# Exponentials of the next attention item placed in the first of two groups; the opening squares and the last rows rearranged

## What is computed

```python
proj = rmsnorm(x, g_in) @ w_in             # split into queries, keys, values, SiLU paths, merge gates
y_a = sliding_window_sink_attention(...)   # 8 heads, window of 2 chunks of 64, a sink logit per head
y_b = sparse_attention(...)                # indexer scores, the 256 best keys of each query, 8 heads
y_c = cross_attention(q, mem keys, mem values)          # 4 heads, 256 keys
u = each y * silu(its z) @ w_branch
merged = sum(sigmoid(gates) * u)
out = rmsnorm(x + merged @ w_out, g_final)
```

## Time and profile before

| | us |
|---|---|
| median of 3 runs (lowest, highest) | 2812.31 (2811.92, 2814.73) |
| the profiled execution | 2818.59 |
| its span, first to last instruction | 2816.8 |
| mean granted TensorE clock, share of full speed | 0.972 |

### The profile page before, as it was taken

The page is one execution under the profiler, slowest core; times in us unless marked ns, Lnnn a source line. Parts: engine busy times, 40 slices in busy tenths (PEclk is TensorE's granted clock), DMA queues, the critical chain, the costliest instruction groups (busy, mean ns, idle before and its releaser), DMA issues.

```text
span 2816.8 us, 37280 instructions
## 1 busy us (share of the span) xinstructions
PE 2528.1 (90%) x13093; PEld 2095.4 (74%) x13093; DVE 1786.0 (63%) x3597; ACT 1372.1 (49%) x2768; POOL 410.3 (15%) x397
## 2 busy tenths in 40 slices
PE   5998999998999999999898999999878888878896
PEld 4776888776778888877677778887667777667785
DVE  6466676225767687227778878622778887777522
ACT  4455645344646444216657445522665673454511
POOL 5334353440000000100000000010000001000010
PEclk9999999999999999999999999999999999999998
DMA  5756584785343522664343511166324333000154
GB/s 162 227 176 213 170 282 150 252 278 183 115 162 119 173 76 68 209 209 155 115 143 104 165 60 53 46 217 206 137 83 149 105 108 132 23 31 31 38 179 165
DMA packets 172537, 399.36 MB, mean 142 GB/s; under 512 B 13760, under 2 KB 96704, under 8 KB 162368
## 3 DMA queue, kind: packets, MB, share of 16 engines
q1 hardware_dynamic: 172352, 396.96, 42.8%
HBM read 308.31 MB, written 88.60 MB: 141 GB/s over the span
## 4 chain that ended last, share of the span: by engine, by line
PE 51%; DVE 21%; ACT 15%; issue 10%; DMA 1%; POOL 1%; SPq 0%; DVEq 0%; ACTq 0%; POOLq 0%
PE bank L861 38%; PE TR L760 5%; PE PV L828 5%; ACT signs L1026 4%; ACT prob L991 3%; ACT prob L1001 3%; DVE ptL L1396 2%; ACT ptH L1015 2%; DVE prob L1355 2%; DVE nmx L1365 2%; DVE score L1617 2%; DVE zs L1427 1%; PE bank L771 1%; PE bank L772 1%; DVE flags L1543 1%
## 5 line engine op out<-in xcount | busy, mean ns | idle before, releaser
L861 PE MATMUL bank<-hH,pairs 128*128 128x512 f32 (+1 forms) x3584 | 1158.5, 393 | 21.0 <-DVE zs L1459 7.6
L861 PEld LDWEIGHTS bank<-hH,pairs 128*128 128x128 f32 x3584 | 679.3, 191 | 160.6 <-issue 22.2
L861 PE MATMUL bank<-hL,pairs 128*128 128x512 f32 (+2 forms) x1792 | 704.1, 393 | 0.0
L1026 ACT ACTIVATE signs<-score,bits 128x384 int8<-128x384 f32 (+7 forms) x256 | 335.8, 1312 | 214.5 <-DVE bits L1497 201.5
L1396 DVE TENSOR_TENSOR ptL<-TR,ptH 128x512 fp32r<-128x512 f32 (+1 forms) x384 | 256.9, 670 | 260.1 <-ACT ptH L1015 256.9
L861 PEld LDWEIGHTS bank<-hL,pairs 128*128 128x128 f32 (+1 forms) x1792 | 343.3, 192 | 65.2
L1015 ACT ACTIVATE ptH<-TR 128x512 fp32r<-128x512 f32 (+1 forms) x384 | 219.6, 576 | 333.6 <-PE TR L760 332.6
L1478 DVE TENSOR_SCALAR_CACHE_REDUCE above<-score,bits 128x256 uint8<-128x256 f32 (+10 forms) x280 | 348.1, 1243 | 9.5
L760 PE MATMUL TR<-identR,prob 128*128 128x128 f32 x1480 | 232.6, 279 | 101.0 <-ACT prob L1001 53.2
L760 PEld LDWEIGHTS TR<-identR,prob 128*128 128x128 f32 x1480 | 178.1, 142 | 178.4 <-ACT prob L1001 66.9
L1176 POOL TENSOR_TENSOR pairs<-raw,pairs 128x512 fp32r<-128x512 f32 x164 | 218.1, 1339 | 316.1 <-ACT pairs L960 315.9
(11 more groups left out here) (206 smaller groups left out, 3636.1 us busy)
## 6 DMA issues: line engine op xcount, KB each, us to landing
pairs<-w_split SPq DMA_DIRECT2D x444, 512.0 KB, 3.5
w_split<-pairs SPq DMA_DIRECT2D x74, 1024.0 KB, 4.9
raw<-in_w_in SPq DMA_DIRECT2D x106, 256.0 KB, 5.6
xs<-in_x SPq DMA_DIRECT2D x4, 2048.0 KB, 9.2
rows<-in_x SPq DMA_DIRECT2D x16, 512.0 KB, 5.2
out<-rows SPq DMA_DIRECT2D x4, 2048.0 KB, 7.5
table<-trig SPq DMA_DIRECT2D x48, 128.0 KB, 2.8
raw<-in_w_branch SPq DMA_DIRECT2D x24, 256.0 KB, 5.6
```

The costliest lines, as they stand in the source:

```text
L861: done = nc.tensor.matmul(PJ[st.u + half * up][0:min(st.width, P), 0:st.n_tok], lhs, rhs[:, row, 0:st.n_tok], start=(n % 12 == 0 and (up o ...
L1026: nc.scalar.activation(signs[:, 0:keys], score[:, tt, 0:keys], ACT.Sign, bias=thr.bitcast(F32)[:, tt:tt + 1], scale=-1.0, accum_out=cnt[:, ...
```

## The change

- `due` returns `[0]` instead of `[ticks - 1]` as the group in which ACT does the next item's exponentials, for branches c and a. ACT's order within an item becomes: ptH of group 0, exponentials of the next item, signs of group 0 (branch a only), woven share, ptH of group 1, signs of group 1, woven share. PE and DVE keep their orders.
- At the start ACT does a small extra square of the identity as soon as that exists, then waits for the memory rows only; the wait for small inputs and the four splits of weights move behind the square root.
- In the last token group the first half of each row tile (channels of out units 0 to 3) is transposed and added after out units 4, 5, 6 and 7, one each. After the last unit the four second halves follow, each with the squares of its tile straight behind it. The final scaling signals tile by tile, and SP stores each tile of 512 KB when it is ready, instead of one store of 2 MB.

```diff
-    def finish_rows(g):
-        steps.append(Step("row_squares", g=g, tr=n["tr"]))
+    def finish_last(g):
+        for tt in range(NT):
+            finish(g, 2 * tt + 1, 2 * tt + 2)
+            steps.append(Step("row_squares", g=g, tr=n["tr"], tt=tt, tiles=1))
         steps.append(Step("row_scale", g=g, tr=n["tr"]))
...
+            if m == KC // 2 - 1:
+                half_out = last_out
             if g + 1 < NG and m < KC - 1:
                 norm("x", g + 1, m + (m > 0), m + 2)
-    finish(NG - 1)
-    finish_rows(NG - 1)
+            elif g + 1 == NG and m >= KC // 2:
+                first = 2 * (m - KC // 2)
+                steps.append(Step("finish", g=g, tr=take("tr"), i=first, evac=half_out.evac))
+    finish_last(NG - 1)
...
             if st.branch != "b":
-                return [0 for _ in after], [ticks - 1]
+                return [0 for _ in after], [0]
...
-                    sp.wait_ge(S["out_ready"], st.g + 1)
-                    sp.dma_start(out_v[st.g], rows[:, :, :]).then_inc(S["store"], 16)
+                    if st.g + 1 < NG:
+                        sp.wait_ge(S["out_ready"], NT * (st.g + 1))
+                        sp.dma_start(out_v[st.g], rows[:, :, :]).then_inc(S["store"], 16)
+                    else:
+                        for t in range(NT):
+                            sp.wait_ge(S["out_ready"], NT * st.g + t + 1)
+                            sp.dma_start(out_v[st.g, :, t, :], rows[:, t, :]).then_inc(S["store"], 16)
...
                     if st.source == "mem":
-                        act.wait_ge(S["small_in"], 16 * (NG + 3))
+                        act.wait_ge(S["consts"], 1)
+                        nc.scalar.activation(squared[:, 0:P], identR[:, :].bitcast(F32), ACT.Square).then_inc(S["squared"], 1)
+                        n_squares[0] += 1
                         act.wait_ge(S["mem_rows_in"], 16)
                     else:
                         act.wait_ge(S["x_in"], 16 * (st.g + 1))
                     squares(nt, tokens)
+                elif st.kind == "scale":
+                    n_root += 1
+                    root(n_root, 0, source_rows(st)[0])
                     if st.source == "mem":
+                        act.wait_ge(S["small_in"], 16 * (NG + 3))
                         for half in range(4):
                             split_hi(half // 2, half % 2)
-                elif st.kind == "scale":
-                    n_root += 1
-                    root(n_root, source_rows(st)[0])
...
                     for t in range(NT):
-                        last = STT(rows[:, t, :], rows[:, t, :], rstd[:, t:t + 1], gfin[:, :], ALU.mult, ALU.mult)
-                    last.then_inc(S["out_ready"], 1)
+                        STT(rows[:, t, :], rows[:, t, :], rstd[:, t:t + 1], gfin[:, :], ALU.mult, ALU.mult).then_inc(S["out_ready"], 1)
```

More of the change, by code:

```diff
@@ L65, in __init__ @@
                  wt=None, u=None, evac=None, used=None, f=None, x=None, y=None, k=None, a=None, tr=None,
-                 p=None, pv=None, scale=None, norm=None, before=None, slots=None, behind=None, woven=None, ring=None):
+                 p=None, pv=None, scale=None, norm=None, before=None, tiles=None, slots=None, behind=None, woven=None, ring=None):
         self.kind = kind
@@ L73, in __init__ @@
         self.tr, self.p, self.pv, self.before, self.slots, self.behind = tr, p, pv, before, slots, behind
+        self.tiles = tiles
         self.scale, self.norm, self.woven, self.ring = scale, norm, woven, ring
@@ L174, in turned @@
         if finishing is not None:
-            steps.append(Step("row_squares", g=finishing, tr=n["tr"]))
+            steps.append(Step("row_squares", g=finishing, tr=n["tr"], tt=0, tiles=NT))
         for role, src, col, more in beside[1:]:
@@ L748, in _ @@
                         sp.dma_start(memkv[:, :].bitcast(F32), mem_scratch).then_inc(S["mem_in"], 16)
-            sp.wait_ge(S["store"], 16 * NG)
+            sp.wait_ge(S["store"], 16 * (NG - 1 + NT))
         @block.tensor
@@ L962, in _, with squares @@
             n_squares = [0]
-            def squares(tiles, src):
-                for t in range(tiles):
+            def squares(tiles, src, first=0):
+                for t in range(first, first + tiles):
                     if n_squares[0]:
@@ L971, in squares, with root @@
                                          accum_out=ssq[:, t:t + 1]).then_inc(S["squared"], 1)
-            def root(n, tiles):
+            def root(n, first, tiles):
                 act.wait_ge(S["var_ready"], n)
-                nc.scalar.activation(rstd[:, 0:tiles], var[:, 0:tiles], ACT.Sqrt).then_inc(S["rooted"], 1)
+                nc.scalar.activation(rstd[:, first:first + tiles], var[:, first:first + tiles], ACT.Sqrt).then_inc(S["rooted"], 1)
             def exps(it, branch, head=0):
@@ L1154, in _ @@
                     act.wait_ge(S["tr_free"], st.tr)
-                    squares(NT, rows)
+                    squares(st.tiles, rows, st.tt)
                 elif st.kind == "row_scale":
                     n_root += 1
-                    root(n_root, NT)
+                    root(n_root, 0, NT)
         @block.gpsimd
@@ L1265, in _ @@
             TT, TS, STT = nc.vector.tensor_tensor, nc.vector.tensor_scalar, nc.vector.scalar_tensor_tensor
-            n_root, n_squares = [0], [0]
+            n_root, n_squares = [0], [1]
             def inverse_rms(tiles):
```

## The result

The changed kernel takes 2852.34 us (median of four runs, 2849.77 to 2854.94) against 2812.11 us before (four runs, 2811.84 to 2814.73): a ratio of 1.0141 [1.0123, 1.0159], 1.4% slower. The forecast was 2850.0 within 2832 to 2862. That is why the spans are 32.6 us apart and the medians 40.2.

A forecast was written before the change was run, and what follows sets the result against it. The prediction took an ACT-DVE ring to bound branches a and c, with PE's wait its shadow. Branch a +28.0, branch c +20.9, start -4.0 and end -7.3 gave +37.6 us, so 2850 us, range 2832 to 2862.

The forecast's parts named there:

- the ring: Branches a and c: closed ACT-DVE loop through signs, ptH, exponentials, maxima and settled bit, setting the pace; 15.3 us per branch-a item.
- Rival A: Branches a and c: PE's wait for exponentials was the bound, so up to 53.2 us is won, 2748 us; chance 5%.
- Branch a: Exponentials moved to group 0: net loss 1.0 us per item with a successor, 28.0 us over four token groups.
- Gain in group 1: Branch a: signs no longer wait for exponentials, only for ptH and DVE's settled bit; gain 0.49 us per item.
- Loss in group 0: Branch a: signs now wait behind exponentials, whose maxima are DVE's last work before the trial value; loss 1.49 us per item.
- Branch c: ptH 1, low half and settled bit now follow the exponentials, delaying the signs; loss 20.9 us, bounds 12 and 24.
- the two full periods: Branch c, second and third of four items: +1.79 us each, 4 x 3.58 us over the token groups.
- the woven gate and split: Branch c, item 1: woven gate (0.47 us, in group 0 with a weight split 1.0) enters the ring; 2.4 us.
- Start: Kernel start: squares begin sooner and the reciprocal comes 3.9 us sooner; gain 4.0 us, bounds 2.0 and 5.4.
- End: Kernel end: squares finish 5.4 us sooner, last store gains 3.0, early transpositions cost 1.1; sum -7.3 us.
- Sum: Whole kernel: 28.0 + 20.9 - 4.0 - 7.3 = +37.6 us, taking the median from 2812.31 to 2850.
- rival C: Branches a and c: PE less busy, lower clock, each of eight stages losing a further 1 to 1.5 us, 2860; chance 9%.

The follow-up runs named there:

- The isolated run: Kernel before with the next item's exponentials moved to group 0 in branch a only: 2843.53 us, ratio 1.0106, +29.1 us.
- The run difference: Kernel before with exponentials moved in branches a and c (2864.43 us) against the same with branch a alone moved (2843.53 us): 20.9 us.

## Why the prediction was right

**Which wait bounds.** The reading that PE's 53.2 us are a shadow of the ring held: taking three of twelve of the woven products away changed nothing (-0.6 us, [-3.7, +1.7] by the ratio's interval), shortening the ring by one reordering on DVE gave -26.5, and lengthening it gave +50.0. Rival A asked for ACT's wait for the trial value to shrink; it did, by 57 us in all, and 121 us of wait for the maxima came instead.

**Branch a, 28.0 us predicted.** Each term has its row. Gain in group 1: 0.49 predicted, and ptH to signs went from 2.36 to 1.87. Loss in group 0: 1.49 predicted, and the signs start 1.49 us behind DVE's trial value. Period in group 3: 16.5 predicted, 16.50 measured in the item shown; in group 0: 12.8 predicted, 12.78 measured (esnk at 288.62 and 301.40). The agreement to the hundredth is the luck of the item: over six periods an item grew by 0.9 us in every token group, where 1.0 was predicted. The stage table has the last seven gains and the last six losses in the stretch of branch a: 4 x (6 x 1.49 - 7 x 0.49) = 22.0, measured 22.7; the first item's loss, 4 x 1.49 = 6.0, lies before the first sign. Of the +4.6 in the table's row ahead of branch a that leaves -1.4 for branch c. The isolated run gave 29.1.

**Branch c, 20.9 us predicted.** The run difference is 20.9. By stages: into branch c +3.9 where 4.2 were expected. In it +17.4 where 14.3 for the two full periods and 2.4 for the woven gate and split stand, 0.7 us short. With the -1.4 branch c comes to 19.9. The sizes by token group, 1.5 for groups 0 and 1 and 0.6 for 2 and 3, were measured as 1.55, 1.57, 0.02 and 0.73. The first two are clear. The last two say little, since this stretch differs by 1.5 us in group 2 and 4.1 in group 3 between kernels that don't change it. Against the kernel with the two ends alone, in place of before, they would be 1.5 and 4.8.

**Start, -4.0 predicted.** The first sign of the program came 4.98 us sooner, and 4.5 sooner than in the kernel with the exponentials' place alone. The reciprocal ran at 9.79 instead of 14.13, 0.46 us sooner than the 10.25 in the sum, since the squares began at 5.92 and not at the 6.35 that I took from the earlier trace rows. Two effects beside POOL's subtractions, which the sum had at 0.1 us together, nearly cancel: from the reciprocal to the scaling is 1.57 us less (2.58 to 1.01), and the scaling takes 1.36 us more (see the last section).

**End, -7.3 predicted.** Measured from the last copy to the span's end: 26.6 us before, 17.8 after, -8.8. Squares gave 5.1 (14.70 to 9.56) where I had 5.4, since each now takes 1.24 us, not 1.18. The store gave 3.6 (11.88 to 8.26) where I had 3.0: quarter stores land in 2.8 us (median), and the span ends 3.3 us after the last one is issued at 2846.04, where I took 4.0. The interleaved transpositions cost more, 0.48 us for each out unit (5.44 to 5.92 from copy to copy) instead of 0.35, three of them 1.4. Net -7.3. The errors in the terms cancel. The Trainium skill's fit (DMA: Bandwidth & Descriptors, Anatomy of one DMA) gave 3.2 us for a 512 KB transfer, nearer to the 2.8 and 3.3 measured than my 4.0.

**Sum.** +37.6 predicted; medians +40.2. What is left is within the uncertainty of the ratio, some 5 us.

**The clock, rival C.** Windows of branch a of group 3 in the changed kernel and in the one with thinner products (busy us of PE, PEld, DVE, ACT and POOL, granted clock, DMA share, GB/s); they answer to the earlier trace rows:

```profile
2220.00:2342.00 122.00, 97.04 (x498) 82.71 (x497) 100.36 (x178) 83.18 (x150) 2.23 (x6) 0.90 0.27 88
```

```profile
2187.00:2309.00 122.00, 92.45 (x473) 79.53 (x472) 108.11 (x193) 89.68 (x151) 3.00 (x8) 0.87 0.28 99
```

The direction of rival C is right: as PE idles more, its granted clock falls, from 0.92 to 0.90 and, with thinner products, 0.87, so more of the stretch is at the lower of the two levels. No cost shows here. The periods are those of the ring without it, and at 0.87 branch a still lasts what it did at 0.92. In group 3 PE has time to spare, idle for 19 of the 122 us before, 25 in the changed kernel and 30 with thinner products. In group 0 it has next to none before, and there the granted clock is 1.00.

## What to carry to other kernels

The longest wait of the busiest engine can be the shadow of a ring between two others: add up one period of that ring from rows before easing the wait, and make the busy engine's work smaller in an experiment, since a period that doesn't move tells that it is not the bound. An instruction moved forward in one engine's queue takes its own wait with it; its price is the time by which its input is later than the work that it now stands in front of, here 1.49 us for exponentials whose maxima are the last thing that DVE makes, and 28 such places are 42 us before the gains (0.49 us for each). The better move was on the side of the producer: publish the small result that the other engine needs (three instructions) ahead of the long work, until the producer itself is full.

## What the runs showed of the hardware

**DVE beside POOL.** In the new start the scaling of the memory rows on DVE lies beside POOL's subtractions and takes twice as long. Before, after the subtractions had ended, and then after:

```profile
11.33 4.93 POOL L1176 TENSOR_TENSOR pairs<-raw,pairs 128x512 fp32r<-128x512 f32 x4
...
14.33 0.73 DVE L1278 TENSOR_TENSOR small<-small 128x2 f32<-128x2 f32 x1
15.09 1.19 DVE L1279 TENSOR_TENSOR small<-small 128x2 f32<-128x2 f32 x1
...
16.71 1.41 DVE L1572 TENSOR_SCALAR mem_rows<-mem_rows,small 128x1024 f32<-128x1024 f32 x2
```

```profile
9.99 0.16 DVE L1294 TENSOR_TENSOR small<-small 128x2 f32<-128x2 f32 x1
10.19 0.16 DVE L1295 TENSOR_TENSOR small<-small 128x2 f32<-128x2 f32 x1
...
10.80 2.77 DVE L1588 TENSOR_SCALAR mem_rows<-mem_rows,small 128x1024 f32<-128x1024 f32 x2
...
11.33 5.82 POOL L1192 TENSOR_TENSOR pairs<-raw,pairs 128x512 fp32r<-128x512 f32 x4
```

POOL's four subtractions took 4.93 us in the kernel before and 5.82 in the changed one, both from 11.33, so POOL is slower too. The longer scaling takes back 1.36 us of the 5.9 that its start gained. The prediction named this without a price. The other side of it is seen in the kernel before: two tiny DVE operations of 128x2 lay beside the same subtractions and took 0.73 and 1.19 us, where they now take 0.16 each. The second ended at 16.28, just behind the last subtraction (16.26). The kernel with the exponentials' place alone shows it again, 0.63 and 1.18 us. No experiment moves POOL's work alone, so that POOL is the cause is read from these times and not shown.

**A store of a quarter.** 2 MB stores of the same rows take 7.5 us from issue to landing (median of three in the changed kernel), 512 KB stores 2.8, loads of x of 512 KB 5.1. The loads lie beside the loads of weights and the stores behind them, so direction and traffic are not told apart. Here the price of a store could not be taken from a load of the same size.
